# The last attention of a two-block network: a pair's query blocks from the fourth down to the first

## What is computed

```python
zlog = jnp.einsum('bqhd,bkhd->bhqk', qi, kp) * scale
log_beta = jax.nn.log_sigmoid(zlog)
log_keep = jnp.where(valid, log_beta - zlog, 0.0)
after = lax.cumsum(log_keep, axis=3, reverse=True) - log_keep
w = jnp.where(valid, jnp.exp(log_beta + after), 0.0)
return jnp.einsum('bhqk,bkhd->bqhd', w, vp)
```

## Time and profile before

| what | value |
|---|---|
| median of 3 runs | 1874.27 us (1873.38 to 1875.89) |
| the profiled execution's own time | 1871.15 us |
| its span, first to last instruction | 1869.4 us |
| TensorE busy | 1723.2 us, 92% |
| VectorE busy | 968.2 us, 52% |
| ScalarE busy | 485.7 us, 26% |
| GpSimd busy | 856.0 us, 46% |
| mean granted TensorE clock | 0.938 of full speed |
| chain that ended last | PE 82%, DVE 12%, ACT 2%, issue 2% |

### The profile page before, as it was taken

One profiled execution on the slowest core, in us unless ns is written; L12 is line 12 of the kernel. 1 busy time (PEld: TensorE's weight loads), 2 busy tenths in 40 slices (PEclk: granted clock), 3 DMA queues, 4 the chain that ended last, 5 costly groups with the idle time before them and its releaser, 6 DMA issues.

```text
span 1869.4 us, 32011 instructions
## 1 busy us (share of the span) xinstructions
PE 1723.2 (92%) x11960; PEld 1500.7 (80%) x11960; DVE 968.2 (52%) x1520; ACT 485.7 (26%) x971; POOL 856.0 (46%) x802
## 2 busy tenths in 40 slices
PE   6899998978999998897898999998897999999996
PEld 2588975866888887897888777775797999999996
DVE  3777215246726663576784776677404655554003
ACT  2211011011026661312223445445312111110001
POOL 0355410335574506174342333331264577777772
PEclk9999989988999999698997999998797899999997
DMA  7356210104220002031110111211132133332331
GB/s 261 100 202 203 82 57 0 44 25 126 76 79 2 2 24 79 23 90 46 46 45 23 46 46 35 55 35 34 28 90 63 56 90 90 90 90 88 94 90 56
DMA packets 208382, 131.34 MB, mean 70 GB/s; under 512 B 5246, under 2 KB 194206, under 8 KB 208174
## 3 DMA queue, kind: packets, MB, share of 16 engines
q1 hardware_dynamic: 208302, 130.21, 23.0%
HBM read 128.10 MB, written 2.10 MB: 70 GB/s over the span
## 4 chain that ended last, share of the span: by engine, by line
PE 82%; DVE 12%; ACT 2%; issue 2%; DMA 1%; SPq 0%; DVEq 0%; POOL 0%; ACTq 0%; POOLq 0%; PEldq 0%
PE ps L1756 20%; PE ps L1757 19%; PE ps L1759 19%; PE ps L1991 2%; PE ps L2246 2%; PE ps L2020 2%; DVE sq L1097 2%; PE ps L1730 2%; PE ps L2187 1%; DVE hp L1129 1%; PE ps L1807 1%; PE ps L1913 1%; PE ps L1741 1%; PE ps L1978 1%; PE ps L2223 1%
## 5 line engine op out<-in xcount | busy, mean ns | idle before, releaser
L644 POOL TENSOR_SCALAR w_hi<-raw 128x512 fp32r<-128x512 f32 x370 | 289.0, 781 | 899.6 <-PE ps L1759 448.0
L646 POOL TENSOR_TENSOR w_lo<-raw,w_hi 128x512 fp32r<-128x512 f32 x370 | 521.7, 1410 | 30.9
L1756 PE MATMUL ps<-op_hi,w_hi 128*128 128x512 f32 x704 | 256.2, 364 | 20.3 <-DVE op_lo L1140 13.3
L1756 PE MATMUL ps<-xn_hi,w_hi 128*128 128x264 f32 x848 | 241.2, 304 | 12.5 <-DVE xn_lo L1138 5.5
L1757 PE MATMUL ps<-op_lo,w_hi 128*128 128x512 f32 x704 | 243.0, 361 | 0.0
L1757 PE MATMUL ps<-xn_lo,w_hi 128*128 128x264 f32 x848 | 227.5, 289 | 0.0
L1759 PE MATMUL ps<-op_hi,w_lo 128*128 128x512 f32 x704 | 211.4, 360 | 0.0
L1756 PEld LDWEIGHTS ps<-xn_hi,w_hi 128*128 128x128 f32 x848 | 162.8, 192 | 46.6 <-issue 37.6
L1756 PE MATMUL ps<-u_hi,w_hi 128*128 128x264 f32 x704 | 190.4, 290 | 8.5 <-DVE u_lo L1651 6.6
L1757 PE MATMUL ps<-u_lo,w_hi 128*128 128x264 f32 x704 | 189.5, 289 | 0.0
L1756 PEld LDWEIGHTS ps<-op_hi,w_hi 128*128 128x128 f32 x704 | 135.5, 192 | 60.0 <-DVE op_lo L1140 12.4
(11 more groups left out here) (299 smaller groups left out, 3081.3 us busy)
## 6 DMA issues: line engine op xcount, KB each, us to landing
raw<-in_w_in SPq DMA_DIRECT2D x45, 512.0 KB, 3.8
raw<-in_w_up SPq DMA_DIRECT2D x44, 512.0 KB, 3.8
ada_ring<-in_ada_w SPq DMA_DIRECT2D x16, 1024.0 KB, 6.3
raw<-in_w_in_ab SPq DMA_DIRECT2D x20, 512.0 KB, 4.1
raw<-in_w_in_c SPq DMA_DIRECT2D x20, 512.0 KB, 3.8
ada_first<-in_ada_w SPq DMA_DIRECT2D x4, 2048.0 KB, 17.3
raw<-in_w_out SPq DMA_DIRECT2D x16, 512.0 KB, 4.0
raw<-in_w_down SPq DMA_DIRECT2D x16, 512.0 KB, 4.0
```

The costliest lines, as they stand in the source:

```text
L644: steps(nc.gpsimd.tensor_scalar(hi, r, 1.0, 0.0, ALU.mult, ALU.add))
L646: nc.gpsimd.tensor_tensor(lo, r, hi.bitcast(F32), ALU.subtract)\
L1756: mm(o[:, 512 * b:512 * b + n], w_h[:, k, :], hi[:, k0 + k, c0:c0 + n], start=a, stop=False)
```

## The change

The blocks of a pair now run from the fourth down to the first, each for both heads, and the two gaps of the bank ring stand before units 16 and 17 instead of 12 and 14. The small block stays in front. The tables that place the chunks, the evacuations and the operand of the output projection stay as they were, by step.

```diff
-        SBU = [(0, 0)] + [(par, blk) for blk in range(1, NT) for par in range(2)]
+        SBU = [(0, 0)] + [(par, blk) for blk in range(NT - 1, 0, -1) for par in range(2)]
...
-        SB_GAPS = (12, 14)
+        SB_GAPS = (16, 17)
```

## The result

The changed kernel takes 1893.82 us (median of 4, 1888.45 to 1899.00), the kernel before, run beside it, 1874.41: ratio 1.0103, 95% interval 1.007 to 1.0136. It is slower, by 19.4 us where 8.7 were forecast, and outside the range of 1877 to 1889. The profiled execution took 1890.8 us (span 1889.0 against 1869.4).

The account below looks back on a forecast made before the run. PE bounds seven of eight pairs, the chain through VectorE, ScalarE and PE the last. Six pairs +7.2, first pair +1.1 and +0.98, large scores +0.5, last pair -1.1: +8.7 on the median 1874.27, 1883.0 us; range 1877 to 1889.

Parts of the forecast that it names:

- the bank ring: Score banks reused in step 2: block 3's scores wait for block 1's output copy; only the longer overlapping wait charged.
- the chain of step 2: VectorE and ScalarE work from V's turning to block 4's first turning: ends at 7.76, PE ready at 6.51; 1.25 us idle.
- M's wait: In step 1, PE idles 0.29 us a pair (0.47 before) for the small block's exponential before turning its weights.
- K's: End of step 7: PE idles 0.37 us (0.26 before) on K's evacuation by ScalarE.
- the wait for 1b's copy: In step 2, PE idle before block 3's first-head scores until block 1's second-head output copy frees their bank: about 1 us.
- the turning of 4a: In step 2, turning the weights of block 4's first head: PE waits about 0.3 us for ScalarE's exponential.
- Steps 3 to 7: Later steps of a steady pair: each turning is wanted later than its chain ends, in step 7 by about 0.1 us.
- the last pair: Without projections to fill PE, its chain was walked from 39.0 to 37.9 us: -1.1, bounds -6 and +2.
- the sum without the clock: The whole forecast: 7.2 + 1.1 + 0.98 + 0.5 - 1.1 = +8.7 us, with no charge for a falling clock.
- the first pair: Its hole before step 2 costs +1.0, K 0.1, and multiplying out block 4's second head itself +0.98 us.
- rival C: Chance 0.15: VectorE dragged into POOL's subtractions (up to 1.27 us a pair) or bubbles lowering PE's clock (2 us); 1891 to 1897.
- A: Chance 0.65: as forecast, one hole a pair in step 2; 1883.0 us, with hole bounds giving 1879 and 1891.

Follow-up runs that it names:

- after_busy1: The changed kernel with a single product of zeros on TensorE ahead of block 3's first scores in step 2; 1885.43 us, ratio 1.0063.
- after_chunks: The changed kernel with five projection chunks in step 2 instead of three, and Q and K evacuated one step sooner; 1892.21 us, ratio 1.0086.

## Why the prediction was right and wrong

**Right: the chain of step 2.** 6.48 us for 6.49 from V's turning to 4a's. M's wait 0.28 for 0.29, K's 0.37 for 0.37, the wait for 1b's copy 1.03 for 1.0. Quick pairs of 37.3 for 37.3 to 37.5. At the turning of 4a itself, where I said 0.3, next to no wait was left (0.89 us from the start of the chunk ahead of it, where a chunk takes 0.73). Steps 3 to 7 had no further wait but K's, and the last pair, from the scores of 4b (1300.99) to the last copy, took 37.1 us, 1.9 less than before, where I said 1.1. No scan met POOL in step 2: scans of 528 elements stayed at 1.25 us.

**Near, with some luck: the sum without the clock.** With the clock kept (after_busy1) the span grew by 9.1 for 8.7, but the terms were further off than that. The start of the stage and the first pair cost 3.2 us where the sum had 2.1, the six pairs 6.6 where it had 7.7, the last pair gave back 1.9 for 1.1, and 1.1 us arose outside the stage, for which it had nothing.

**Wrong: "Against it: 0.73 us a pair did not move the clock from 1.00"**, the step by which rival C got 0.15 with POOL and clock together, and A 0.65. The old order's rest was in pieces of 0.47 and 0.26 in the steady pairs; the new one's had a piece of 1.03 close behind one of 0.28, and a price for it could not be read off pieces less than half its size. A row that bore on it was there: in the last pair the clock had gone to 0.50 by 1290 though no wait had been longer than 1.23 us, if with less work between the waits, since that pair has no chunks.

```profile
1287.92 0.39 PE L2223 MATMUL ps<-ident,sb_sum 128*16 128x128 f32 x2 [1.23 <-ACT sb_sum L1044]
1288.24 0.94 PE L2187 MATMUL ps<-ks,qs 64*128 64x400 f32 x2
1289.99 0.81 PE L2223 MATMUL ps<-ident,sb_sum 128*16 128x128 f32 x3 [0.82 <-ACT sb_sum L1044]
```

I used the fall of the last pair for that pair and not for the others. So the sum had nothing for the clock, where the runs show 10.0 us. The range then stopped at 1889, short of A's own bound of 1891 and of C's 1891 to 1897, in which the result lies, though it was said to take in both A's bounds and the near half of C. C's term, 2 us a pair, was of the right size for a fall: five falls in seven pairs cost 10.0 us, 1.4 us a pair. Of its two mechanisms it was the clock. The Trainium skill, TensorE: Matmul & The Clock Gate, section on a second failure mode, says of another kernel that brief idling between groups of matrix products made the clock swing between its two levels. The trace agrees (0.99, then 0.50 behind the hole).

**Half right: the bank ring.** "The new gaps cost nothing more" holds for the time of a pair. But the ring turned the hole into a wait of 1.03 us in one piece, and after_chunks shows that it, not the exponential, has to be covered first.

**Not settled.** Which pairs fall. The lengths 40.2, 38.7, 37.3 come twice in a row in the changed kernel, with one and the same hole in all six, so the fall depends on more than the hole. Nor does the length of the wait decide: with 1.03 us two pairs of the changed kernel kept their clock, the first lost it behind 0.75, after_busy1 kept it with 0.80 to 0.82, and one execution of after_chunks, at 1884.28 us, is too short for the five falls of its profiled one (1893.27). So no length of wait that is safe can be read from these runs. Whether four banks' distance for the fourth blocks could be had with other gaps was not tried. Why executions reach the stage at two times was not followed.

## What to carry to other kernels

A hole on TensorE can cost twice: itself, and the half clock behind it. Where an edit opens a wait of about a microsecond in a stage that had only short ones, put the clock into the sum and the range, and look for rows of the same kernel in which it fell. And cover a wait with work that stands ahead of the first wait in the engine's order; a table of how much work a step has says nothing without where in the step it stands.

## What the chip showed that was not expected

Work without a result, only there to keep the clock, saved 10 to 11 us of stage: with five products of zeros 317.2 became 307.2, and the profiled execution with a single one, 0.22 us, has 306.1. The clock fell at the hole's end or up to 0.9 us behind it, so the loss shows as longer products behind it and not as idle time: PE's busy share stayed at 92% on the page before and after.
